# A step order for a recurrent mixer: gate and keys issued as steps of their own, and convolution taps spread evenly

## The reference

```
h = x @ w_in ;  a_u, a_v, a_g, b_val, b_glu, b_g, c_q, c_f, c_i, c_g = split(h)
y_a = sgu(gelu(a_u), layernorm(gelu(a_v))) * silu(a_g)
y_b = silu(layernorm(conv31(b_val * sigmoid(b_glu)))) * silu(b_g)
# recurrence, per head: f = lb + (1 - lb) sigmoid(c_f);  k = 1 - f;  q = silu(c_q)
#   S_t = diag(f_t) S_{t-1} + k_t outer i_t ;   o_t = S_t^T q_t ;   o = rmsnorm(o) * norm_g
y_c = o * silu(c_g)
x1 = layernorm(alpha * x + concat(y_a, y_b, y_c) @ w_out)
```

## Time and profile before

| | us |
|---|---|
| median of 3 runs (lowest, highest) | 3722.06 (3717.59, 3725.05) |
| the profiled execution, its time | 3724.5 |
| its span, first to last instruction | 3722.8 |
| PE busy | 3518.2 (95%) |
| PE weight loads busy (beside PE) | 2937.1 (79%) |
| DVE busy | 2152.4 (58%) |
| POOL busy | 1738.0 (47%) |
| ACT busy | 1154.7 (31%) |
| mean granted TensorE clock | 0.980 of full |

### The profile page before, as it was taken

The page is one execution under the profiler, slowest core; times in us unless marked ns, Lnnn a source line. Parts: engine busy times, 40 slices in busy tenths (PEclk is TensorE's granted clock), DMA queues, the critical chain, the costliest instruction groups (busy, mean ns, idle before and its releaser), DMA issues.

```text
span 3722.8 us, 51933 instructions
## 1 busy us (share of the span) xinstructions
PE 3518.2 (95%) x22042; PEld 2937.1 (79%) x22042; DVE 2152.4 (58%) x2745; ACT 1154.7 (31%) x1919; POOL 1738.0 (47%) x1248
## 2 busy tenths in 40 slices
PE   7999998988999999999898999989999899999998
PEld 6878877877778787877777888777788787877876
DVE  7754566467364545456874466637778355454545
ACT  2122112357222222223122122236666222222223
POOL 4222432639355545555332332533388345545455
PEclk9999999999999999999999999999999999999999
DMA  3101312554201111113111132261222210111011
GB/s 123 36 24 35 142 51 85 183 146 128 82 23 46 57 46 57 46 57 136 41 41 35 35 147 83 99 220 58 69 91 58 80 35 34 68 35 68 35 68 63
DMA packets 79690, 275.82 MB, mean 74 GB/s; under 512 B 9057, under 2 KB 9313, under 8 KB 76900
## 3 DMA queue, kind: packets, MB, share of 16 engines
q1 hardware_dynamic: 70816, 242.25, 19.5%
q10 hardware_dynamic: 8642, 30.24, 2.1%
HBM read 224.23 MB, written 48.23 MB: 73 GB/s over the span
## 4 chain that ended last, share of the span: by engine, by line
PE 72%; DVE 17%; ACT 4%; issue 3%; POOL 3%; DMA 0%; POOLq 0%; SPq 0%; DVEq 0%; ACTq 0%
PE ps L1411 19%; PE ps L1412 19%; PE ps L1413 19%; PE ps L1417 4%; DVE acc L2108 3%; PE ps L1711 2%; PE ps L1681 2%; PE ps L1682 2%; PE ps L1716 2%; DVE tf_lo_p L2107 2%; DVE af_hi_p L2107 1%; ACT wd_hi L1765 1%; DVE af_lo_p L2107 1%; PE ps L1486 1%; DVE px L2107 1%
## 5 line engine op out<-in xcount | busy, mean ns | idle before, releaser
L2692 POOL TENSOR_TENSOR ring_lo<-ring_raw,ring_hi 128x512 fp32r<-128x512 f32 (+1 forms) x356 | 599.6, 1690 | 383.4 <-ACT ring_hi L1765 373.8
L1411 PE MATMUL ps<-a_hi,ring_hi 128*128 128x512 f32 x1472 | 590.9, 401 | 29.4 <-DVE af_hi_p L2107 16.3
L1412 PE MATMUL ps<-a_lo,ring_hi 128*128 128x512 f32 x1472 | 577.9, 393 | 0.0
L1413 PE MATMUL ps<-a_hi,ring_lo 128*128 128x512 f32 x1472 | 577.4, 392 | 0.0
L1411 PEld LDWEIGHTS ps<-a_hi,ring_hi 128*128 128x128 f32 x1472 | 279.0, 190 | 104.0 <-DVE af_hi_p L2107 23.9
L1413 PEld LDWEIGHTS ps<-a_hi,ring_lo 128*128 128x128 f32 x1472 | 278.9, 189 | 60.1
L1412 PEld LDWEIGHTS ps<-a_lo,ring_hi 128*128 128x128 f32 x1472 | 279.4, 190 | 54.4
L2107 DVE TENSOR_TENSOR xres<-xres,ps 128x512 f32<-128x512 f32 x352 | 234.9, 684 | 149.8 <-PE ps L1413 147.6
L1411 PE MATMUL ps<-wd_hi,af_hi 128*128 128x512 f32 x704 | 277.9, 395 | 23.4 <-DVE xres L2107 17.5
L1412 PE MATMUL ps<-wd_lo,af_hi 128*128 128x512 f32 x704 | 276.6, 393 | 0.0
L1765 ACT ACTIVATE ring_hi<-ring_raw 128x512 fp32r<-128x512 f32 (+1 forms) x286 | 180.5, 635 | 309.1 <-PE ps L1413 195.9
(11 more groups left out here) (305 smaller groups left out, 8075.5 us busy)
## 6 DMA issues: line engine op xcount, KB each, us to landing
ring_raw<-w SPq DMA_DIRECT2D x92, 512.0 KB, 3.5
ring_raw<-wgu SPq DMA_DIRECT2D x68, 512.0 KB, 3.7
uq<-q_scr SPq DMA_DIRECT2D x96, 256.0 KB, 4.7
ring_raw<-wd SPq DMA_DIRECT2D x34, 512.0 KB, 3.6
ring_raw<-wo SPq DMA_DIRECT2D x32, 512.0 KB, 3.7
uk<-k_scr SPq DMA_DIRECT2D x6, 2048.0 KB, 10.7
rlf<-wgu SPq DMA_DIRECT2D x20, 512.0 KB, 4.6
xraw<-xt SPq DMA_DIRECT2D x16, 512.0 KB, 7.2
```

What stands on the lines that cost most here:

```text
L1411: pe.matmul(o, ah, bh, start=begin and i == 0, stop=False)
L1412: pe.matmul(o, ah, bl, start=False, stop=False)
L1413: last = pe.matmul(o, al, bh, start=False, stop=end and i == len(pairs) - 1)
L2692: tt = lambda o, a, b, op: pool.tensor_tensor(o, a, b, op=op)
```

## The change

Five edits, all in both halves. (1) The gate is a step `hg_gate` and the keys are a step `hg_keys`; both are emitted once f of the head has left PE, followed by two turns, and only then is q waited for. The gate of the next head may be emitted in one of the three turns behind `hg_out`. (2) At level 7 `kb` is multiplied before `qb`; `hg_out` gets a semaphore for `qb` (`hg_q`). (3) `conv` ends its turn after two of three taps (before: after every other tap) until q0 is begun, and after four of five (before: after every tap) from then on. (4) Two more turns stand ahead of the first `conv_turn`, and two more ahead of the first `conv_fin`. (5) What follows from it, since `hg_fin` 1 waits for `conv`: heads 2 and 3 come several dense steps later, and `sgu_norm` takes another place.

```diff
         def hgrn():
             emit("hg_zero", hf, begin)
+            gated = 0
             for h in range(4):
-                while not (until(f"f{h}", 2) and until(f"q{h}", 2)):
+                while not until(f"f{h}", 2):
+                    yield False
+                if gated == h:
+                    emit("hg_gate", hf, h)
+                    gated += 1
+                emit("hg_keys", hf, h, begin)
+                yield True
+                yield True
+                while not until(f"q{h}", 2):
                     yield False
...
                 for _ in range(3):
                     yield True
+                    if gated == h + 1 < 4 and until(f"f{h + 1}", 2):
+                        emit("hg_gate", hf, h + 1)
+                        gated += 1
...
-                if n % 2 or "q0" in ev:
+                if n % (5 if "q0" in ev else 3):
                     yield True
             emit("conv_hist", hf)
+            for _ in range(2):
+                yield True
             for tp in range(4):
...
             emit("conv_norm", hf)
             ydone.add("st")
-            yield True
+            for _ in range(3):
+                yield True
...
             elif kind == "hg_out":
-                for mark in new("pe", [("hg_sc64", hf, h)]):
+                for mark in new("pe", [("hg_sc64", hf, h), ("hg_q", hf, h)]):
...
+            if l == 7:
+                tt(kv, kv, tv[:, :, 1]...).then_inc(*up("hg_lv", hf, h, l))
+                tt(qv, qv, tv[:, :, 0]...).then_inc(*up("hg_q", hf, h))
+                return
```

More of the change, by code:

```diff
@@ L46 @@
     ("act_mixer", "late_exp late_rw late_b2 hg_sc32 hg_sc64 hg_kt hg_o hg_keep hg_sq conv_ct conv_silu"),
-    ("dve_hgrn", "late_dve late_nlam hg_f hg_k hg_pick hg_lv hg_state hg_sum hg_normed hg_y hg_lo"),
+    ("dve_hgrn", "late_dve late_nlam hg_f hg_k hg_pick hg_lv hg_q hg_state hg_sum hg_normed hg_y hg_lo"),
     ("dve_conv", "val tap conv_stats conv_mean conv_normed conv_cy conv_lo"),
@@ L2141, in level @@
                 dve.wait_ge(*at(*mark))
+            if l == 7:
+                tt(kv, kv, tv[:, :, 1].unsqueeze(2).to_broadcast([128, n, c]), ALU.mult).then_inc(*up("hg_lv", hf, h, l))
+                tt(qv, qv, tv[:, :, 0].unsqueeze(2).to_broadcast([128, n, c]), ALU.mult).then_inc(*up("hg_q", hf, h))
+                return
             tt(qv, qv, tv[:, :, 0].unsqueeze(2).to_broadcast([128, n, c]), ALU.mult)
@@ L2218, in vector @@
                 tt(o, PS[b][:, :], o, ALU.mult).then_inc(*up("val", hf, name, c))
+            elif kind == "hg_gate":
+                hf, h = a
+                fb = FB[h % 2]
+                for mark in new("dve", [("evac", hf, f"f{h}", 1)]):
+                    dve.wait_ge(*at(*mark))
+                if h == hf == 0:
+                    for mark in new("dve", [("late_nlam",)]):
+                        dve.wait_ge(*at(*mark))
+                dve.tensor_scalar(fb[:, :], fb[:, :], OML[:, h:h + 1], LB[:, h:h + 1], op0=ALU.mult, op1=ALU.add
+                                  ).then_inc(*up("hg_f", hf, h))
+            elif kind == "hg_keys":
+                hf, h, begin = a
+                for mark in new("dve", [("hg_f", hf, h)]):
+                    dve.wait_ge(*at(*mark))
+                if h:
+                    for mark in new("dve", [("hg_back", hf, h - 1, 1)]):
+                        dve.wait_ge(*at(*mark))
+                else:
+                    for mark in new("dve", begin["kb"]):
+                        dve.wait_ge(*at(*mark))
+                dve.tensor_scalar(KB[:, :], FB[h % 2][:, :], -1.0, 1.0, op0=ALU.mult, op1=ALU.add
+                                  ).then_inc(*up("hg_k", hf, h))
             elif kind == "hg_level":
@@ L2223, in vector @@
                 if l == 0:
[L2224 to L2239, removed]
                     if h:
```

## The result

| | before | after |
|---|---|---|
| median of 4 runs each, us (lowest, highest) | 3723.56 (3717.59, 3725.22) | 3688.96 (3687.42, 3696.26) |
| ratio to before, 95% interval | | 0.9913 (0.9897 to 0.9929) |
| span of the profiled execution | 3722.8 | 3685.7 |
| PE waits in 20 to 480 us (half 0) | 27.4 | 14.0 |
| mean granted TensorE clock of that execution | 0.980 | 0.987 |

The changed kernel is 34.6 us faster by the medians; by the ratio it is 32 us, with an interval of 26 to 38. It was forecast at 3696 with a range of 3682 to 3712; the forecast gain was 26.8, so it lies inside that interval. Three executions of later runs, one of e5 and two of e7, took 5797 to 8888 us, and the medians and ratios leave them out.

A forecast was written before the change was run, and what follows sets the result against it. PE, busy 95% of the span, was taken as the bound, so gains come only from its waits and clock. Terms of -13.4 us a half, -26.8 in both, gave 3696 us, with 3682 to 3712 for 8 in 10.

The forecast's parts named there:

- Head 0: First scores of head 0: PE's 9.63 us wait for keys becomes 1.75; with the clock -10.2 us a half.
- Head 1: Head 1: waits of 0.75 for q, 4.1 at level 1 and 1.2 at level 4; with clock +4.8 us a half.
- Levels: Level steps where every fifth turn holds two taps: cost 0, bound 0 to +1.5 us.
- Head 2: Head 2: 1.6 us of wait for keys goes, 1.2 for kb is left; with clock -3.1 us a half.
- Head 3: Head 3: SGU norm ahead of the state updates makes a new 3.6 us wait; with other terms +2.4 us a half.
- Keys first: Level 7: PE can turn kb 0.6 us sooner, but no row of it waits there: 0.
- The first turn of `acc`: Convolution: a dense step later, 2.7 us of PE work, cuts the 5.0 us wait to 2.3.
- The clock terms: Parts of the forecast for PE's lower clock behind waits: -2.1 + 1.7 - 2.0 - 0.7 + 1.0 = -2.1 us a half.
- rival on the clock: Short waits may each bring the lower clock as long ones do, so only waits count: 3700 us, chance 0.05.
- Half the gain given back: DVE late at more levels, waits of 1 to 4 us in heads 1, 3 and at acc: 3710 us, chance 0.2.
- More gain: The normalising takes 2.67 us and head 1's wait is 1: -20.6 us a half, 3681 us, chance 0.13.
- The slower one: DVE steps with paired taps and a split take 6.6 us against PE's 3.76, at most levels: slower than before, chance 0.06.

The follow-up runs named there:

- e5: The changed kernel with the later convolution turns undone (turns as early as before): 3716.9 us, ratio 0.9983 to the kernel before.
- e7: The changed kernel with gate and keys put back behind q, at the head of level 0: 3709.9 us, ratio 0.9968 to the kernel before.
- e8: The changed kernel with the SGU norm held back until the output of head 3 is issued: 3680.5 us, ratio 0.9888 to the kernel before.
- e4: The changed kernel with the queries multiplied first again in the last level: 3689.6 us, ratio 0.9918 to the kernel before.
- e2: The kernel before with the new tap spacing alone (two of three, then four of five taps end a turn): 3720.6 us, ratio 1.0006.
- e3: The kernel before with the later convolution turns alone (two more ahead of the first turns of acc and ct): 3716.0 us, ratio 0.9991.
- e6: The changed kernel with the tap spacing undone (taps spaced as before): 3708.7 us, ratio 0.9963 to the kernel before.
- e11: The changed kernel with conv_hist, POOL's copy of the convolution's history, behind the two added turns: 3697.3 us, ratio 0.9939 to the kernel before.
- e1: The kernel before with gate and keys as steps of their own, taps and convolution turns as before: 3721.2 us, ratio 1.0003.

## Why the prediction was right, point by point

*Head 0* was right in place and size: 9.63 and 10.04 became 0.94 (forecast 1.75). *Head 1*: forecast 0.75, 4.1 and 1.2, measured 0.78, 4.47 and 1.55; the step that a split falls on the taps whole is seen in 8.97 us for five. *Levels*: pairs of taps cost nothing, as said. *Head 2*: 1.2 forecast, 1.23 measured. *Head 3*: 3.6 forecast, 3.57 measured, behind a normalising of 8.38; e8 takes the cause away and the wait goes. *Keys first*: nothing, by e4.

One term was mis-sized. The first turn of `acc` was put at 2.3 us left; it was 0. The prediction moved PE's side of this wait, by a dense step, and left DVE's side as it was, with 6.5 us for the last three taps. The PE side was right: counted in the traces, the first turn stands 12 matmuls earlier by the spacing (e2, e5) and 24 later by the added turns (e3, e6), 12 later in all. But the spacing also brings `conv_hist` ahead of a weight split on POOL, and the three taps, free of it, take 2.9 us less. e11 puts the split back ahead of `conv_hist`, and the wait is 2.32 us, just what the prediction had left. In e6 the taps take 6.59 us and PE waits nothing, because its turn comes 12 matmuls later than in the changed kernel.

Over the two profiled executions, waits in the halves fell by 13.4 and 13.7 us, 27.1 in all; the prediction's terms without clock add up to 22.0. Of the 5.1 between, 4.6 are the turn of `acc`. PE is 31.9 us ahead over the two halves (16.3 and 15.6), so 4.8 us came from work that ran faster. The clock terms add up to the same 4.8 (the prediction's rival on the clock has 2.1 a half, leaving out the 0.3 of head 3; it is 2.4). That these microseconds come from the clock is likely, since the granted clock rose from 0.98 to 0.99 in half 0 and from 0.97 to 0.99 in half 1, but no run shows it apart, and that the two sums agree to the tenth is luck: a stretch that nobody edits varies by more. The rest of the 37.1 us between the two spans is such scatter, since outside the halves no edit is made, and PE's waits there even grew (over the whole span they fell from 191.4 to 167.2, by 24.2 and not 27.1).

Of the rivals, none came. Half the gain given back wanted waits of 1 to 4 us at more levels and again at the turn of `acc`, which waited nothing. More gain wanted a normalising of 2.67 us and a wait of 1 us in head 1; they were 8.38 and 4.47. The slower one did not come near. The prediction would have called itself wrong at a wait at four or more levels: half 0 has 0.16, 4.47, 1.55 and 1.23, so by the letter this sign is there, though the first is too small to count.

What the prediction did not say is how the gain hangs together. It went place by place, with all edits in place at once, and so never needed the worth of one edit; read edit by edit, its terms would mislead. The wait of head 0 goes by the spacing alone (e2), only to come back at head 1, and by e1 to e3 and e5 to e7 no edit has a worth of its own that could be added to the others'.

## What to carry to other kernels

Where one engine has a backlog of filler work (here 62 taps on DVE) between pieces that another engine waits for, ask at how many places the backlog meets the other engine; moving it past one shows up at the next, and several edits that are each worth nothing may be worth 0.9% together. When a step moves in a list that all engines walk, redo the row of every engine around its new place, POOL's small copies included. In these traces filler on DVE that ran beside a weight split on POOL took up to 2.9 us longer for each split; look where those stand before choosing its place.

## What the runs showed of the hardware

A normalising of eight instructions on DVE took 2.67 us with no POOL split beside it, 5.58 with one and 8.38 with two: 2.8 to 2.9 us for a split whose own two-input instruction takes 2.34 to 2.40. The keys of head 0, one instruction on 128x1024, took 2.76 us from 70.84 on, beside a split, and those of e1 0.69 with none. These DVE instructions have one full tensor as input, so not only those with two are held up. The Trainium skill (SBUF — State Buffer, SBUF: two separate sides) counts among VectorE's operations that exclude GpSimd those in a mode that uses both ports; that this is such a mode no run here shows.
